# The weight ring of the experts: two lent slots given up, four kept

## The chip, the cores and the metric

One core of a Trainium2 chip runs the whole program. The metric is the device time of one execution in microseconds (us); less is better.

## The reference, cut to what matters

The program computes two transformer-like blocks over 512 tokens of width 1024. The first block has two layers, and each layer ends in an expert stage:

```python
def expert_choice_moe(h, w_router, w_gate, w_up, w_down):
    cap = EC_FACTOR * s // N_EXPERTS                 # 2 * 512 // 16 = 64 tokens for each expert
    logits = jnp.einsum('bsd,de->bse', h, w_router)
    aff = jax.nn.softmax(logits, axis=-1)
    gates, idx = lax.top_k(aff.transpose(0, 2, 1), cap)
    xs = h[b_ix, idx]                                # 64 tokens of each of the 16 experts
    a = jnp.einsum('becd,edf->becf', xs, w_gate)     # 1024 x 1024, float32
    u = jnp.einsum('becd,edf->becf', xs, w_up)       # 1024 x 1024
    y = jnp.einsum('becf,efd->becd', jax.nn.silu(a) * u, w_down)   # 1024 x 1024
    y = y * gates[..., None]
    return jnp.zeros_like(h).at[b_ix, idx].add(y)
```

Each expert has three matrices of 1024 x 1024 in float32, 4 MB each: a layer reads 16 x 3 x 4 MB = 192 MB (of 2^20 bytes) of expert weights, and each weight serves only 64 tokens. The other stages of the program (projections, attention, a recurrent mixer, a long convolution, a feed-forward net) are not touched by the change.

## The kernel before, in words

**Weights come in pieces.** `weight_pieces` writes down all weights of the first block in the order of their use, in pieces of at most 2048 KB. An expert has six pieces: two of `w_gate`, two of `w_up`, two of `w_down`; here they are called G0, G1, U0, U1, D0, D1. A layer has 96 of them. Experts are counted from 0 to 15.

**A ring holds them.** `Ring` (line 51) owns `RING` = 4 slots of 16 KB in each partition, one piece to a slot. `feed` (line 76) runs on SP, the engine whose queue issues the loads. For each next piece it takes the slot whose last piece is the oldest, waits until that piece is used, and issues the load:

```python
s = min((s for s in range(len(self.tiles)) if i < self.until[s]), key=lambda s: self.last[s])
if self.last[s] >= self.fed:
    break
if self.last[s] >= 0:
    sp.wait_ge(self.used, self.last[s] + 1)
sp.dma_start(self.tiles[s][:, 0:src.shape[1]], src).then_inc(self.landed[s], 16)
```

So the loads are issued strictly in the order of the pieces, and a stage's `feed` goes on to the pieces of the next stage as far as the slots let it. `take` makes TensorE wait until a piece has landed; `done` raises `used` with the last matmul that reads the piece.

**Two slots are lent.** The expert stage (`Experts.run`, line 1378) allocates `LENT` = 2 further tiles `lent_weights` and hands them to the ring with `ring.lend(lent, ring.fed + 6 * NE)` (line 1390), until the 96 pieces of the layer are through. With six slots and six pieces to an expert, D0 and D1 always fall into the lent tiles, and G0 to U1 into the ring's own. When the stage begins, the own four slots have already been filled by the stage before (G0 to U1 of expert 0).

**What TensorE does in an expert** (its order is written out by hand in `run`): G0 (`project`, line 1476), the spreading of the places (line 1468), G1, then U0 and U1 and, between them, the put-back of the previous expert's rows (line 1509), the turn of the hidden rows (line 1484), D0 (`down`, line 1495), then the picks of the next group's tokens (line 1451), then D1. Experts come in groups of four. The picks for the next group are spread over a group: two blocks of picks in its first expert, three in the second and third, none in the fourth, which has the slot columns (line 1460) in their place. The last group has neither. Before the first expert the stage has a part that needs no expert weights: softmax, choice of the 64 tokens on VectorE, and the picks of the first group.

After layer 0's experts, the next stage (`chain`, lines 438 to 584) takes the pieces of `w_in` of layer 1. After layer 1's experts the first ring ends; the second block has a ring of its own, `weight_ring_second`, with `RING_2` = 2 slots.

Of the kernel before, what the change touches and what calls it, by code (L numbers as in the profile page):

```python
# [43 lines left out]
CHUNK = 64  # L44
NCH = T // CHUNK
DECAY = -math.exp(-0.5)
RING, RING_2, LENT = 4, 2, 2
SLOT_COLS = 512


# [2890 lines left out]
```

## Time and profile before

| | us |
|---|---|
| median of three runs | 4118.49 (4117.94 to 4123.21) |
| the profiled execution, its own time | 4114.72 |
| its span in the profile | 4113.4 |
| expert weights of layer 0 in use by TensorE | about 523 to 978 |
| expert weights of layer 1 in use by TensorE | about 1493 to 1948 |

TensorE is busy for 86% of the span. The DMA engines are busy for 37% of it on the average, but unevenly: nearly all in two stretches, those of the expert weights. The table's last two lines are positions in the profiled execution, counted from the start of the span.

### The profile page before, as it was taken

How to read it: one execution, taken by the hardware profiler on the slowest of the kernel's cores; microseconds unless marked ns; L12 is line 12 of the kernel's file. 1: busy time of each engine (PE TensorE's matmuls, PEld its weight loads, DVE VectorE, ACT ScalarE, POOL GpSimd, SP SyncE). 2: the span in 40 equal slices, each digit the busy share in tenths (PEclk: the TensorE clock that was granted, in tenths of full speed). 3: DMA queues.
4: the chain of work that ended last, by engine and by line, in shares of the span. 5: the costliest groups of instructions: out<-in, count | busy, mean ns of one | idle time of the engine just before them, and what ended most of it. 6: DMA issues, size and time to landing. Idle time of an engine off the chain costs nothing. (4 is left out here: it accounts for less than half of the span.)

```text
span 4113.4 us, 54317 instructions
## 1 busy us (share of the span) xinstructions
PE 3528.7 (86%) x22946; PEld 2340.4 (57%) x22946; DVE 1963.4 (48%) x2907; ACT 1113.0 (27%) x1839; POOL 310.6 (8%) x248
## 2 busy tenths in 40 slices
PE   7689799998689979998777666578999998789998
PEld 6377443334457643332556555435888776368887
DVE  3655423224365432322455665525764542867645
ACT  3343200002163310000321222112433421554333
POOL 1010000000010000000102332000000100210000
PEclk9899899999899989999888777879999998899999
DMA  5021289997113159998220000001222221422221
GB/s 193 11 103 62 84 366 427 427 428 302 53 42 116 49 224 427 427 428 375 104 78 3 2 2 2 2 33 67 103 103 87 78 103 44 63 76 102 83 92 72
DMA packets 79487, 600.99 MB, mean 146 GB/s; under 512 B 35304, under 2 KB 36584, under 8 KB 43981
## 3 DMA queue, kind: packets, MB, share of 16 engines
q1 hardware_dynamic: 79244, 597.51, 37.0%
q8 instruction: 182, 2.98, 0.3%
q14 instruction: 61, 0.49, 0.0%
HBM read 595.39 MB, written 2.10 MB: 145 GB/s over the span
## 5 line engine op out<-in xcount | busy, mean ns | idle before, releaser
L574 PE MATMUL psum<-source_hi,weights_hi 128*128 128x512 f32 (+1 forms) x2352 | 923.2, 393 | 105.1 <-DVE weights_lo L486 81.0
L574 PE MATMUL psum<-source_lo,weights_hi 128*128 128x512 f32 (+1 forms) x2352 | 913.2, 388 | 0.0
L574 PE MATMUL psum<-source_hi,weights_lo 128*128 128x512 f32 (+1 forms) x2352 | 911.9, 388 | 0.0
L574 PEld LDWEIGHTS psum<-source_hi,weights_hi 128*128 128x128 f32 x2352 | 449.7, 191 | 207.2 <-DVE weights_lo L486 96.2
L574 PEld LDWEIGHTS psum<-source_lo,weights_hi 128*128 128x128 f32 x2352 | 450.3, 191 | 90.0 <-issue 2.7
L574 PEld LDWEIGHTS psum<-source_hi,weights_lo 128*128 128x128 f32 x2352 | 449.6, 191 | 90.2
L1476 PE MATMUL psum<-weight_ring_first,branches 128*64 128x512 f32 x2048 | 465.5, 597 | 16.4 <-DMA weight_ring_first<-in_w_gate 8.6
L486 DVE TENSOR_TENSOR weights_lo<-weight_ring_second,weights_hi 128x1024 fp32r<-128x1024 f32 (+3 forms) x230 | 285.4, 1245 | 301.2 <-ACT weights_hi L441 301.1
L1476 PEld LDWEIGHTS psum<-weight_ring_first,branches 128*64 128x64 f32 x2048 | 138.0, 137 | 304.7 <-issue 270.8
L441 ACT CAST weights_hi<-weight_ring_second 128x1024 fp32r<-128x1024 f32 (+3 forms) x230 | 228.3, 997 | 267.5 <-PE psum L574 244.7
L1627 DVE TENSOR_TENSOR x<-psum,x 128x512 f32<-128x512 f32 x256 | 164.1, 684 | 202.2 <-PE psum L1509 202.2
L1495 PE MATMUL psum<-lent_weights,hidden_t 128*64 128x512 f32 x1024 | 233.7, 598 | 3.3 <-DMA lent_weights<-in_w_down 1.6
L486 DVE TENSOR_TENSOR weights_lo<-weight_ring_first,weights_hi 128x1024 fp32r<-128x1024 f32 (+2 forms) x112 | 140.4, 1269 | 168.4 <-ACT weights_hi L441 168.4
L538 POOL TENSOR_TENSOR sums_of_squares<-squares 128x512 f32<-128x512 f32 (+1 forms) x16 | 25.5, 1596 | 2079.1 <-ACT squares L459 2079.1
L2267 ACT ACTIVATE convolved<-before_convolution,columns 128x512 f32<-128x512 f32 x88 | 71.9, 817 | 277.2 <-DVE before_convolution L2264 277.2
L441 ACT CAST weights_hi<-weight_ring_first 128x1024 fp32r<-128x1024 f32 (+2 forms) x112 | 111.0, 1011 | 131.7 <-PE psum L574 124.3
L1495 PEld LDWEIGHTS psum<-lent_weights,hidden_t 128*64 128x64 f32 x1024 | 67.9, 136 | 135.8 <-issue 109.6
L1987 PE MATMUL psum<-rwkv_scratch 64*64 64x64 f32 x3584 | 114.6, 227 | 22.4 <-POOL rwkv_scratch L1978 22.4
L1987 PEld LDWEIGHTS psum<-rwkv_scratch 64*64 64x64 f32 x3584 | 113.9, 144 | 23.1 <-POOL rwkv_scratch L1978 22.9
L574 PE MATMUL psum<-weights_hi,source_hi 128*128 128x256 f32 x384 | 110.7, 288 | 10.0 <-DVE weights_lo L486 10.0
L2264 DVE TENSOR_TENSOR before_convolution<-psum,roots 128x512 f32<-128x512 f32 x100 | 68.9, 689 | 103.4 <-PE psum L574 103.3
L574 PE MATMUL psum<-weights_hi,source_lo 128*128 128x256 f32 x384 | 110.0, 286 | 0.0
(359 smaller groups left out, 4584.5 us busy)
## 6 DMA issues: line engine op xcount, KB each, us to landing
weight_ring_first<-in_w_gate SPq DMA_DIRECT2D x64, 2048.0 KB, 18.0
weight_ring_first<-in_w_up SPq DMA_DIRECT2D x64, 2048.0 KB, 19.1
lent_weights<-in_w_down SPq DMA_DIRECT2D x64, 2048.0 KB, 18.2
weight_ring_second<-in_ffn_w_up SPq DMA_DIRECT2D x22, 2048.0 KB, 8.0
weight_ring_first<-in_xattn_w_kv SPq DMA_DIRECT2D x8, 2048.0 KB, 8.1
weight_ring_second<-in_ffn_w_down SPq DMA_DIRECT2D x8, 2048.0 KB, 8.0
weight_ring_first<-in_w_in SPq DMA_DIRECT2D x6, 2048.0 KB, 24.4
weight_ring_second<-in_mix_w_in SPq DMA_DIRECT2D x6, 2048.0 KB, 8.0
```

Source lines behind the costliest of these rows:

```text
L441: act.copy(self.whi[:, 0:len(unit.ks), unit.slot * P:unit.slot * P + unit.cols], self.ring.view(unit.piece)[:, :, unit.c0:unit.c0 + unit.c ...
L486: ins = dve.tensor_tensor(lo, self.ring.view(unit.piece)[:, :, unit.c0:unit.c0 + unit.cols], hi.bitcast(F32), ALU.subtract)
L538: pool.tensor_tensor(total, square(q) if m == 1 else total, square(q + m), ALU.add).then_inc(self.added, 1)
L574: ins = pe.matmul(ps, a, b, start=k == 0 and q == 0, stop=k == job.rows // P - 1 and q == 2)
L1476: ins = pe.matmul(psum[HALF * half:HALF * half + HALF, which, :], self.xs[:, k, e // GROUP % 2, e % GROUP * CAP:(e % GROUP + 1) * CAP], w[ ...
L1495: ins = pe.matmul(psum[HALF * half:HALF * half + HALF, self.ROWS, :], hid_t[:, k, part * HALF:(part + 1) * HALF], w[:, k, half * 512:half ...
L1627: dve.tensor_tensor(x, psum[:, bank(), :], x, ALU.add).then_inc(misc_free, 1)
L1987: ins = pe.matmul(K.psum[r, bank + d, c], w[d][r, lhs, c], w[d][r, rhs, c], start=True, stop=True)
L2264: return dve.tensor_tensor(self.raw[:, m % 3, :], ps, r[0], ALU.mult)
L2267: act.activation(self.to(m), self.raw[:, m % 3, :], ACT.Identity, bias=self.b[:, m:m + 1], scale=self.w[1][:, m:m + 1]).then_inc(self.cent ...
```

## The change

The ring borrows nothing any more. `lent` becomes an empty list, `lend` does nothing, and all pieces go through the four own slots. In the expert stage the load of a piece waits for the piece four places before it, where it waited for the one six places before it; and the loads of D0 and D1 of expert 0, which needed no wait, now wait for G0 and G1.

```diff
-RING, RING_2, LENT = 4, 2, 2
+RING, RING_2, LENT = 4, 2, 0
```

Nothing else is edited: every engine's order of computing instructions stays as it is.

## Rows read from the trace of the kernel before

**Rows 1.** The page: span, TensorE, and GB/s in 40 equal slices.

```profile
span 4113.4 us, 54317 instructions
...
GB/s 193 11 103 62 84 366 427 427 428 302 53 42 116 49 224 427 427 428 375 104 78 3 2 2 2 2 33 67 103 103 87 78 103 44 63 76 102 83 92 72
```

**Rows 2.** The page's DMA issues: count, KB each, median us to landing.

```profile
lent_weights<-in_w_down SPq DMA_DIRECT2D x64, 2048.0 KB, 18.2
```

**Rows 3.** Busy time by stretch: us, PE, PEld, DVE, ACT, POOL, PEclk, DMA share, GB/s.

```profile
500.00:520.00 20.00, 9.82 (x59) 9.74 (x60) 12.46 (x26) 0.00 (x0) 0.00 (x0) 0.58 0.00 1
540.00:560.00 20.00, 19.48 (x94) 7.49 (x96) 3.69 (x6) 1.74 (x3) 0.00 (x0) 1.00 1.01 429
800.00:900.00 100.00, 97.75 (x522) 36.52 (x520) 26.27 (x42) 6.43 (x11) 0.00 (x0) 1.00 1.01 428
900.00:950.00 50.00, 44.01 (x204) 13.93 (x202) 13.76 (x21) 3.46 (x6) 0.00 (x0) 1.00 1.01 428
```

**Rows 4.** Timeline of SP's queue, layer 0: start, us, line, load, count.

```profile
486.82 0.91 SPq L84 DMA_DIRECT2D lent_weights<-in_w_down  x2
526.79 4.96 SPq L84 DMA_DIRECT2D weight_ring_first<-in_w_gate  x2
...
553.31 4.96 SPq L84 DMA_DIRECT2D weight_ring_first<-in_w_gate  x2
562.19 4.58 SPq L84 DMA_DIRECT2D weight_ring_first<-in_w_up  x2
572.35 6.92 SPq L84 DMA_DIRECT2D lent_weights<-in_w_down  x2
582.38 4.96 SPq L84 DMA_DIRECT2D weight_ring_first<-in_w_gate  x2
...
953.57 15.25 SPq L84 DMA_DIRECT2D weight_ring_first<-in_w_in  x4
```

**Rows 5.** Timeline of TensorE in layer 0, early: start, us, line, matmuls, count.

```profile
540.52 3.65 PE L1495 MATMUL psum<-lent_weights,hidden_t 128*64 128x512 f32 x16 [0.68 <-ACT hidden_t L1589]
...
582.27 1.12 PE L1468 MATMUL psum<-place_rows,row_selectors 16*128 16x512 f32 x2
...
591.81 3.65 PE L1476 MATMUL psum<-weight_ring_first,branches 128*64 128x512 f32 x16
...
696.30 1.12 PE L1468 MATMUL psum<-place_rows,row_selectors 16*128 16x512 f32 x2
```

**Rows 6.** Timeline of TensorE, experts 14 and 15 of layer 0; in brackets its idle time.

```profile
920.52 3.65 PE L1476 MATMUL psum<-weight_ring_first,branches 128*64 128x512 f32 x16 [1.25 <-DMA weight_ring_first<-in_w_gate]
...
949.88 3.65 PE L1476 MATMUL psum<-weight_ring_first,branches 128*64 128x512 f32 x16 [1.24 <-DMA weight_ring_first<-in_w_gate]
...
974.59 3.65 PE L1495 MATMUL psum<-lent_weights,hidden_t 128*64 128x512 f32 x16 [0.23 <-DMA lent_weights<-in_w_down]
```

**Rows 7.** The same view, D1 of expert 15 in layer 1.

```profile
1944.84 3.65 PE L1495 MATMUL psum<-lent_weights,hidden_t 128*64 128x512 f32 x16 [0.20 <-DMA lent_weights<-in_w_down]
```

**Rows 8.** Ring and lent slots' loads issued in 520:560, in that order.

```profile
DMA to landing us min/median/max: 8.1/11.2/12.2
DMA to landing us min/median/max: 10.6/10.8/11.0
```

**Rows 9.** Lent slots' loads issued in 560:600, ring slots' in 600:650 and 900:950.

```profile
DMA to landing us min/median/max: 10.9/11.8/12.6
...
DMA to landing us min/median/max: 12.9/14.5/16.3
...
DMA to landing us min/median/max: 25.6/25.6/25.9
```

**Rows 10.** Waits in 840:880, those for a DMA: us in total, times, longest.

```profile
PEld psum L1476 <- DMA weight_ring_first<-in_w_up: 0.4, 1, 0.4
```

**Rows 11.** Timeline after the experts of layer 0, ScalarE: the next stage's first cast.

```profile
986.49 1.03 ACT L441 CAST weights_hi<-weight_ring_first 128x1024 fp32r<-128x1024 f32 x1
```

## The prediction, on record before the run

> **What bounds the kernel now.** I read the page first, for where the DMA engines matter at all. Its line of GB/s has two plateaus at 427 to 428, each about five slices of 103 us wide, and elsewhere mostly under 200 [rows 1]. The plateaus are the two expert stages; the change can act only there, for only there are slots lent [rows 2].
>
> Second, the busy times by stretch [rows 3]. In every stretch from 540 us on, the DMA share is 1.01 and the rate 428 or 429: the DMA engines are full from the first expert to the last. TensorE is nearly full too at 800:900, but at 900:950 it is busy for only 44 of 50 us. From 500 to 520 the DMA engines do nothing: all slots are full and the tokens are still being chosen.
>
> Third, the timeline of TensorE at both ends of the stage [rows 5, 6]. The places of expert 2 are spread at 582.27 and those of expert 6 at 696.30: a group of four takes 114.03 us, and TensorE waits for no load in it. The list of waits shows the first, of 0.4 us, only in 840:880 [rows 10]. In the last group, which has no picks, G0 of experts 14 and 15 start at 920.52 and 949.88, each behind a wait for its load. So an expert takes 29.36 us there, and a piece 29.36 / 6 = 4.893 us: that is the DMA engines' pace, to be read off TensorE. Four experts at this pace are 117.4 us. TensorE alone is 3.4 us a group faster; it begins with a stock of pieces landed ahead, eats it up over the first three groups, and is held by the loads in the last. D1, the last piece, starts at 974.59 behind a wait of 0.23 us for its landing; in layer 1 the same stands at 1944.84, with 0.20 us [rows 6, 7]. **The end of both expert stages is thus the landing of the 96th piece**, and that is set by when the stream begins and how many pieces it still has to carry.
>
> **The change, part by part.**
>
> *The head start.* Before, D0 and D1 of expert 0 are issued at 486.82 and land in the idle time; six pieces lie ready when G0 starts. The next load is issued at 526.79, when G0 is used [rows 4]. From then the stream carries 96 - 6 = 90 pieces of the layer. After the change D0 and D1 can't be issued at 486.82. The load at 526.79 is then D0's, the next is D1's, and the stream carries 92 pieces. Two pieces more at 4.893 us are **9.79 us** for a layer, and 19.57 us for both. The idle time at 500:520 can't take them back, since no slot is free.
>
> *Does TensorE wait for D0 of expert 0?* It needs it at 540.52 [rows 5]. The first load of the stream lands in 8.1 us (the minimum [rows 8]), at 534.9. Nothing is lost here.
>
> *Does a ring of four keep the DMA engines full?* SP issues a load in the moment a piece is used; the timeline gives those moments. A row of two loads starts with the first, and the second starts at the row's end less its own 0.33 us. For expert 1: G0 553.31, G1 557.94, U0 562.19, U1 566.44, D0 572.35, D1 578.94, and expert 2's G0 582.38 [rows 4]. As long as TensorE isn't held, these moments are the same after the change, so the stream is the same too, only with each transfer two pieces further back in the list. A load issued when piece i is used brings piece i+4, and TensorE has the time until it wants i+4. The shortest is for D1 of expert 1: used at 578.94, its slot brings U1 of expert 2, wanted at 591.81 [rows 5], 12.87 us. The transfers issued in 560:600 to the lent slots take at most 12.6 us, those in 600:650 12.9 and more [rows 9]. So the first waits come around 590 to 620 us, in experts 2 and 3, and not at 840. From there on TensorE is held to the DMA engines' pace.
>
> Is that pace still 4.893 us? The engines run dry only if a slot comes free too late. Suppose U1 starts as it lands, at about 562.8 in the moments above. The next three landings of the stream are D0's at 567.7, D1's at 572.6 and G0's at 577.5. D1, delayed by the picks, is used at 578.94, some 6.3 us after it landed. The load that this releases has to land 4 x 4.893 = 19.6 us after D1 did, at 592.2, so it has 13.2 us. A load into an empty queue needs 8.1, and at 540:560, where loads take 10.6 to 12.2 us, the share is already 1.01 [rows 3, 8]. There are at least 5 us in hand at the worst place. Cost: nothing. If this cover were gone, each late release would cost its lateness.
>
> *The wait at the end.* In the last group the loads take 25.6 us now, since six slots queue up before the engines [rows 9]. With four it should be 25.6 - 9.8 = 15.8 us. The queue is shorter and the pace is the same.
>
> *The next stage.* SP's waits change the other loads too. Before, the four pieces of w_in are issued from 953.57 on, behind G0, G1, U0, U1 of expert 15 [rows 4]. Now they wait for U0, U1, D0, D1. The first of them lands right behind D1 of expert 15: that one lands at 974.6 + 9.8 = 984.4, the next at 989.3. The next stage's first cast of it comes at 986.49 [rows 11], moved to 996.3: 7 us of cover. The three others are released by U1, D0 and D1, and come one by one while ScalarE is still at the first; the fourth, released at 984.4 + 3.65 = 988.0, lands 8.1 us after at the earliest. Cost: nothing, with the bound that a late fourth piece would be under 10 us. Nothing else is queued behind SP's waits, for the two small tables are issued ahead of them. In layer 1 no piece follows in this ring.
>
> *The pace itself.* The rate is 429 at the short queue of 540:560 and 428 with the long one of 900:950 [rows 3]. At best the short queue wins 1/428 of 450 us, 1 us a layer; at worst a wait on TensorE costs some tenths at the end. I take neither.
>
> Sum: 4114.72 (the profiled execution; its span is 4113.4, with 1.3 us around it) + 19.57 = 4134.3 us. The median of the runs shown is 3.77 us above the profiled execution, so on that median it is 4118.49 + 19.57 = **4138.1 us**, 0.48% slower.
>
> **The rule that speaks against this.** In the last group the rows show TensorE with a wait for nearly each load though six slots are there [rows 6]. The Trainium skill, "Trainium Kernel Development and Optimization", section "Best Practices", asks for double buffering so that DMA and compute overlap; by it, a ring of four pieces is already twice what is needed, and the sum would be 4118.5. The trace disagrees with its being enough here: loads and matmuls overlap all the way, and the end still moves with the number of pieces that were landed ahead. "SBUF — State Buffer", section "The DMA setup-cost knee", of the Trainium skill gives a lone transfer a fixed cost of about 2 us beside bytes over 436 GB/s; as an estimate from that page that is 6.8 us for 2 MB, where the trace has 8.1. The sum is the same by both.
>
> **The rivals.**
>
> *The two slots are hidden anyway (same).* TensorE's own work would have to end the stage: it would have to be at least 9.8 us behind the loads at D1 of expert 15. The 98% of busy time at 800:900 speaks for it. The waits at all of the last group's experts, and the 0.2 us waits at D1 in both layers, speak against it [rows 6, 7]: there is no slack at the end to put 9.8 us into. It would give 4118.5. The point that decides: the landing of D1 has to lie at least 9.8 us before its use, and it lies at it. This is the case on the other side, not slower; I give it 3%.
>
> *The ring of four runs dry.* If the three picks made one release in each expert come so late that its load finds an empty queue, that load costs 8.1 - 4.9 = 3.2 us more than its share. In 14 experts of a layer that is 45 us, 90 in both: 4138 + 90 = 4228 us. It decides when a piece is used more than 11.5 us after its landing (three landings of 4.9, less the 3.2); the worst I find is 6.3. If only the three or four experts around the start of the waits did it, 3 us each, it would be 4138 + 20 = 4158. 5% for the two.
>
> *The next stage pays too.* If the cast at 996.3 had to wait for pieces of w_in, some 5 us once: 4143. Inside the range, 5%.
>
> *Faster.* A shorter queue would have to raise the rate by 9.8 of 450 us, 2.2%, to 437 GB/s, to break even; the row with the shortest queue shows 429. 1%, for something that I don't see.
>
> **How the numbers follow.** The forecast, 4138, has 86%. A change within 0.2% (8 us) is about what a measurement of this kernel can't tell from none. Slower by more is the forecast with the dry ring and the late next stage: 96%; same 3%, faster 1%. The range: low is the lowest run, 4117.9, plus the sum less the 2 us that a better rate might bring, 4135.5, taken down to 4133 for another chip; high is the highest run, 4123.2, plus 19.6 and the late next stage, 4148.
>
> **What the profile after would show.** No lent_weights. In each layer the first load of the stage 40 us later, at TensorE's first release, and the last D1 9.8 us later than before, at about 984.4. The first wait for a load near 600 instead of 870. Waits for loads in all later groups, of 0.3 to 1.3 us, and experts at 29.36 us each from the second group on. Loads in the last group at 15.8 us, and never under 10 after the first few. The DMA share at 1.01 and 427 to 429 GB/s throughout. The end of the program 19.6 us later, and all between and behind the expert stages as long as before. It would be wrong if the share fell under 1 in the groups with picks (ring dry), or if D1 of expert 15 started without a wait (hidden).

## The result, and the profile after

The changed kernel takes 4139.72 us in the median, the kernel before 4117.40 us over all its runs: a ratio of 1.0052, with a 95% interval of 1.0040 to 1.0064. It is slower, as forecast (4138.1 us, 1.0048). One of its six executions took 8938.04 us, and one of the five of its repeat below 6968.64; the ratios leave these two slow ones out, the medians given hold them, and without them the medians are 4137.98 and 4135.50 us. The profiled execution has its own time of 4136.37 us and this span and rates, the answer to [rows 1]:

```profile
span 4135.0 us, 54317 instructions
...
GB/s 192 11 102 62 43 371 427 427 428 307 72 41 102 62 170 427 427 428 419 102 79 2 2 2 2 3 33 66 102 86 93 87 102 44 63 75 94 90 92 72
```

The plateaus stand at 427 to 428 as before; what changed is their edge. The slice before the first plateau fell from 84 to 43 GB/s and that before the second from 224 to 170, and more is moved behind them: the loads that used to lie in the idle time are in the stream now.

The queue of SP in the changed kernel, layer 0 and then layer 1, in the columns of [rows 4]:

```profile
487.56 0.42 SPq L1427 DMA_DIRECT2D places<-in_places  x1
527.97 4.96 SPq L84 DMA_DIRECT2D weight_ring_first<-in_w_down  x2
...
975.54 15.23 SPq L84 DMA_DIRECT2D weight_ring_first<-in_w_in  x4
...
1507.57 4.96 SPq L84 DMA_DIRECT2D weight_ring_first<-in_w_down  x2
```

Behind the two small tables nothing is issued for 40 us; D0 and D1 of expert 0 go out at TensorE's first releases. In the kernel before, the stream of layer 1 began here:

```profile
1496.15 4.96 SPq L84 DMA_DIRECT2D weight_ring_first<-in_w_gate  x2
```

TensorE in the changed kernel: its first wait for a load in layer 0, G0 of experts 14 and 15, D1 of expert 15, and the same D1 in layer 1, to be held against [rows 5, 6, 7]:

```profile
645.93 3.65 PE L1476 MATMUL psum<-weight_ring_first,branches 128*64 128x512 f32 x16 [0.28 <-DMA weight_ring_first<-in_w_up]
...
932.69 3.65 PE L1476 MATMUL psum<-weight_ring_first,branches 128*64 128x512 f32 x16 [1.24 <-DMA weight_ring_first<-in_w_gate]
...
962.07 3.65 PE L1476 MATMUL psum<-weight_ring_first,branches 128*64 128x512 f32 x16 [1.24 <-DMA weight_ring_first<-in_w_gate]
...
986.75 3.65 PE L1495 MATMUL psum<-weight_ring_first,hidden_t 128*64 128x512 f32 x16 [0.23 <-DMA weight_ring_first<-in_w_down]
...
1965.60 3.65 PE L1495 MATMUL psum<-weight_ring_first,hidden_t 128*64 128x512 f32 x16 [0.20 <-DMA weight_ring_first<-in_w_down]
```

An expert of the last group lasts 962.07 - 932.69 = 29.38 us, and 29.36 before: the same pace, the same gaps of 1.24 us at G0. The last D1 starts 12.16 us later in layer 0 and 20.76 us later in layer 1.

Busy time by stretch, with the columns of [rows 3]:

```profile
500.00:520.00 20.00, 8.63 (x49) 8.55 (x50) 12.95 (x28) 0.00 (x0) 0.00 (x0) 0.55 0.00 1
540.00:560.00 20.00, 18.96 (x92) 7.47 (x94) 2.94 (x6) 1.86 (x3) 0.00 (x0) 1.00 1.01 431
800.00:900.00 100.00, 95.52 (x516) 36.14 (x514) 28.07 (x45) 6.17 (x10) 0.00 (x0) 1.00 1.01 428
900.00:950.00 50.00, 44.33 (x198) 13.67 (x196) 11.28 (x17) 3.13 (x5) 0.00 (x0) 1.00 1.01 428
```

The DMA share is 1.01 in each stretch behind the start, as with six slots. At 800:900 TensorE is busy for 95.5 us and not for 97.8: it is held there now. The granted clock is 1.00 in both. Over 400 us of the first stream, the kernel before and then the changed one, the DMA columns are the same and only TensorE's differ:

```profile
560.00:960.00 400.00, 388.54 (x2017) 143.18 (x2014) 114.95 (x187) 26.04 (x42) 0.00 (x0) 1.00 1.01 427
560.00:960.00 400.00, 381.18 (x1980) 140.75 (x1978) 113.75 (x185) 24.77 (x40) 0.00 (x0) 1.00 1.01 427
```

Times from issue to landing of the loads issued in 600:650 and in 900:950, the answer to [rows 9]:

```profile
DMA to landing us min/median/max: 12.2/14.2/17.2
...
DMA to landing us min/median/max: 14.8/15.8/15.9
```

**Where the 21.6 us of span are.** I take as the length of a stream the time from the first load after expert 0's G0 to the start of the last D1. Layer 0: 974.59 - 526.79 = 447.80 us before, 986.75 - 527.97 = 458.78 after, 10.98 more. Layer 1: 1944.84 - 1496.15 = 448.69 before, 1965.60 - 1507.57 = 458.03 after, 9.34 more. Together 20.3 us. The rest of the program has 1.3 us more: 1.18 ahead of the first stream, -0.74 between the two, 0.84 behind the second.

### The profile page after: what moved, and what is told of

Same layout as the page of the kernel before. It is cut to its first block and busy times, and to the rows that moved or that the text cites. A ratio compares the mean times of both kernels' runs of the same rounds, so it can differ in the third digit from the quotient of the medians.

```text
span 4135.0 us, 54317 instructions
## 1 busy us (share of the span) xinstructions
PE 3533.9 (85%) x22946; PEld 2340.4 (57%) x22946; DVE 1959.9 (47%) x2907; ACT 1113.0 (27%) x1839; POOL 310.7 (8%) x248
## 5 line engine op out<-in xcount | busy, mean ns | idle before, releaser
L1495 PE MATMUL psum<-weight_ring_first,hidden_t 128*64 128x512 f32 x1024 | 233.7, 598 | 3.5 <-DMA weight_ring_first<-in_w_down 1.8
L1495 PEld LDWEIGHTS psum<-weight_ring_first,hidden_t 128*64 128x64 f32 x1024 | 67.8, 136 | 136.1 <-issue 109.6
L574 PE MATMUL psum<-weights_lo,source_hi 128*128 128x256 f32 x384 | 110.0, 287 | 0.0
## 6 DMA issues: line engine op xcount, KB each, us to landing
weight_ring_first<-in_w_gate SPq DMA_DIRECT2D x64, 2048.0 KB, 15.8
```

The costliest lines, as they stand in the source:

```text
L574: ins = pe.matmul(ps, a, b, start=k == 0 and q == 0, stop=k == job.rows // P - 1 and q == 2)
L1495: ins = pe.matmul(psum[HALF * half:HALF * half + HALF, self.ROWS, :], hid_t[:, k, part * HALF:(part + 1) * HALF], w[:, k, half * 512:half ...
```

## The experiments

The theory: the end of an expert stage is the landing of its last piece; the DMA engines are full from TensorE's first release on; so each piece that isn't loaded in the idle time ahead costs 4.9 us a layer. Rivals: four slots are too shallow to keep the engines full, or each wait of TensorE costs something in itself. All eight kernels of the experiments were timed in five rounds beside the kernel before, the first four in one set and the last four in another; the first row of the table has the ratio of the result above. The sum of the two streams is 447.80 + 448.69 = 896.5 us for the kernel before and 458.78 + 458.03 = 916.8 for the changed one.

| kernel | ratio to before (95%) | sum of both streams, us | over before |
|---|---|---|---|
| kernel before | 1 | 896.5 | 0 |
| changed kernel | 1.0052 (1.0040 to 1.0064) | 916.8 | 20.3 |
| the same again | 1.0047 (1.0033 to 1.0060) | 918.5 | 22.0 |
| one lent slot | 1.0029 (1.0019 to 1.0040) | 907.6 | 11.1 |
| six slots, no head start | 1.0048 (1.0034 to 1.0061) | 915.2 | 18.7 |
| four slots, four halves in expert 8 | 1.0017 (1.0008 to 1.0025) | 902.1 | 5.6 |
| four slots, halves spread | 1.0001 (0.9992 to 1.0010) | 899.0 | 2.5 |
| lent for two loads only | 1.0034 (1.0023 to 1.0044) | 911.1 | 14.7 |
| six slots, shared tiles | 1.0002 (0.9993 to 1.0011) | 897.6 | 1.1 |
| three lent slots | 0.9970 (0.9959 to 0.9981) | 888.8 | -7.7 |

**The changed kernel again.** No edit.

> The changed kernel once more, beside the kernels of this call. Theory (the end of an expert stage is the landing of its last piece, and two pieces more have to be carried after the first release): 19.6 us slower than before, ratio 1.0048; from the first load after expert 0's G0 to the last D1 458 to 459 us in each layer, where six slots have 448. Rival (the measured 1.0052 came from the chip or from work outside the expert stages): a ratio within 0.2% of 1.

Measured: 4136.07 us, ratio 1.0047 (1.0033 to 1.0060). The loss is reproduced, and the rival falls. In layer 1 the stream is 458.2 us (1512.23 to 1970.42), in layer 0 460.4 (530.84 to 991.19). The same kernel had 458.8 there, so one profile tells a stream's length to some 1.6 us. In layer 0 of the repeat one row differs: U0 of expert 15 waits 2.13 us for its load and its matmuls take 5.35 us in place of 3.65, and D1 then follows D0 without a wait. What delayed that load isn't shown.

**One lent slot.**

```diff
-RING, RING_2, LENT = 4, 2, 2
+RING, RING_2, LENT = 4, 2, 1
```

> One lent slot in place of two: five pieces lie ready when expert 0 starts. Theory: one piece of 4.9 us more in each stream than with two, so 9.8 us slower than before, ratio 1.0024, and D1 of expert 15 4.9 us later than with two lent slots in each layer; loads of the last group take 20.7 us. Rival (a ring of four has its loss from too few transfers in flight, and five are enough): ratio within 0.0005 of 1 and no shift of D1.

Measured: 4128.33 us, ratio 1.0029 (1.0019 to 1.0040), the interval holding the 1.0024 of the theory and not the rival's 1.000. SP's first loads of the two streams, and the last D1 of both layers:

```profile
525.16 0.33 SPq L84 DMA_DIRECT2D weight_ring_first<-in_w_down  x1
...
1501.41 0.33 SPq L84 DMA_DIRECT2D weight_ring_first<-in_w_down  x1
```

```profile
979.17 3.65 PE L1495 MATMUL psum<-weight_ring_first,hidden_t 128*64 128x512 f32 x16 [0.24 <-DMA weight_ring_first<-in_w_down]
...
1955.00 3.65 PE L1495 MATMUL psum<-weight_ring_first,hidden_t 128*64 128x512 f32 x16 [0.20 <-DMA weight_ring_first<-in_w_down]
```

454.0 and 453.6 us, 6.2 and 4.9 more than with two lent slots. The price goes by the piece: about half the loss for half the slots. The load of the lent slot goes out alone here, at 485.19 behind the two small tables, with no other for 40 us. Its time to landing:

```profile
DMA to landing us min/median/max: 8.1/8.1/8.1
```

**Six slots without the head start.** The lent slots are told that they last held the stage's first piece, so their first loads wait until it is used.

```diff
 def lend(self, tiles, until):
-        self.tiles[self.own + i], self.last[self.own + i], self.until[self.own + i] = tile, -1, until
+        self.tiles[self.own + i], self.last[self.own + i], self.until[self.own + i] = tile, self.fed, until
```

> Six slots as before, but the two lent ones stay empty until expert 0's G0 is used; the depth of the ring is that of before from then on, only the two pieces that were loaded in the idle time are missing. Theory (head start): as slow as four slots, 19.6 us over before, ratio 1.0048, and 458 us from the first load to the last D1. Loads of the last group at 25.6 us as with six slots. Rival (depth of the queue): as fast as before, ratio 1.000.

Measured: 4136.11 us, ratio 1.0048 (1.0034 to 1.0061), the number of the theory. SP's queue at the start of layer 0's stream (three loads at once, as two slots more come free with the first piece), then the loads issued in 600:650, their time to landing:

```profile
526.48 0.33 SPq L84 DMA_DIRECT2D weight_ring_first<-in_w_down  x1
526.86 0.43 SPq L84 DMA_DIRECT2D lent_weights<-in_w_down  x1
527.33 0.43 SPq L84 DMA_DIRECT2D lent_weights<-in_w_gate  x1
```

```profile
DMA to landing us min/median/max: 22.2/23.1/24.8
```

Loads take 23.1 us at 600:650, where the kernel before has 14.5 and the changed one 14.2: two pieces more are queued before the engines. And nothing is won by it. This is the run that separates the two things that a lent slot does: more depth than four slots have is worth nothing here, the load in the idle time is worth the whole difference. The streams are 458.1 and 457.1 us. In layer 0 D1 follows D0 without a wait here too, behind a row of U0 of 5.35 us; in layer 1 it waits 0.19 us for its load.

**Four slots and two pieces' worth of bytes fewer.** The four loads of gate and up weights of expert 8 bring half of their bytes; the other half of the slot keeps older weights, so expert 8 is computed partly with stale ones. TensorE's work is whole.

```diff
+            cut = src.shape[1] // 2 if i in self.halved else src.shape[1]
-            sp.dma_start(self.tiles[s][:, 0:src.shape[1]], src).then_inc(self.landed[s], 16)
+            sp.dma_start(self.tiles[s][:, 0:cut], src[:, 0:cut]).then_inc(self.landed[s], 16)
...
             ring.lend(lent, ring.fed + 6 * NE)
+            ring.halved += tuple(ring.fed + 6 * 8 + j for j in range(4))
```

> Four slots, and the four loads of expert 8's gate and up weights bring only half of their bytes (the other half of the slot keeps what lay there, so expert 8 is computed with partly stale weights): the stream carries two pieces' worth less, as with the head start. TensorE does all its matmuls. Theory (the number of bytes between the first release and the last landing sets the end): D1 of expert 15 back where it was with six slots, 448 us after the first load, and the time of before, ratio 1.000 within 0.0007. Rival (the ring of four loses time at late releases or in each wait of TensorE): most of the 19.6 us stay, ratio 1.003 to 1.005.

Measured: 4122.81 us, ratio 1.0017 (1.0008 to 1.0025), between the two expectations, and neither holds: 14.7 us of stream came back, 5.6 stayed. The trace shows where. Busy time at 740:760, and the shortest, median and longest time to landing of the loads issued in 750:800:

```profile
740.00:760.00 20.00, 19.72 (x150) 7.95 (x150) 6.18 (x13) 1.77 (x3) 0.00 (x0) 1.00 0.94 364
```

```profile
DMA to landing us min/median/max: 6.5/10.1/12.3
```

The halved loads brought the stream 9.8 us ahead of TensorE at once. Four slots can't hold such a lead: no slot came free in time, the queue ran short, and the DMA share fell to 0.94. That is the dry ring of the prediction, brought about by the edit. (The 6.5 us is a halved load's, issued at 751.3; the whole piece behind it, issued at 754.7, took 8.1.)

**The same bytes taken where TensorE can follow.** Only G0 of experts 11 to 14 is halved (those four are computed with partly stale gate weights).

```diff
-            ring.halved += tuple(ring.fed + 6 * 8 + j for j in range(4))
+            ring.halved += tuple(ring.fed + 6 * e for e in (11, 12, 13, 14))
```

> Four slots, two pieces' worth of bytes fewer once more, now taken where TensorE is held by the loads and can catch up by 3.2 us an expert: only G0 of experts 11, 12, 13 and 14 is loaded by half (these experts are computed with partly stale gate weights). In the run before this one the four halved loads stood together in expert 8, the time to landing fell to 6.5 us there and the DMA share to 0.94: the ring ran dry and 5.6 of 20 us stayed. Theory: with the cuts spread the queue never empties, the DMA share stays at 1.01, and all of the two pieces comes back: 448 us from the first load to the last D1, ratio 1.000 (0.9993 to 1.0010). Rival (the rest of 5.6 us is a loss of four slots in itself): ratio 1.0013 or more.

Measured: 4118.13 us, ratio 1.0001 (0.9992 to 1.0010). With four slots, and with TensorE's waits and late releases in place up to the first halved load, taking two pieces' worth of bytes out of the stream gives the time of the kernel before. Behind expert 11 most of the waits are gone with the bytes: at 900:950 TensorE is busy for 49.2 us, where the changed kernel has 44.3. So for the waits ahead of it this run shows no cost; those behind it aren't tested by it. By the streams 2.5 us of 20.3 remain, 1.9 in layer 0 and 0.6 in layer 1, where two profiles of one kernel differed by 1.6 in a layer; the rival's 1.0013 is outside the interval.

**Lent slots for two loads only.** The lent slots take D0 and D1 of expert 0 and are given back.

```diff
-            ring.lend(lent, ring.fed + 6 * NE)
+            ring.lend(lent, ring.fed + 6)
```

> The two lent slots carry D0 and D1 of expert 0 and nothing more; from the seventh piece on all goes through the own four. So the head start of before is there and the depth isn't: the load of piece 10 is released by piece 6 and not by piece 4, some 9 us later than with six slots, when the queue is already empty. Theory (a head start lasts only if slots hold it): between the two: 86 pieces behind a load issued at about 553 end at 978, 3 us later than before, and some holes of 1 to 3 us while the queue is short; 8 to 12 us slower in all, ratio 1.0020 to 1.0030, with a DMA share under 1 between 545 and 600. Rival A (only the head start counts): ratio 1.000. Rival B (only the depth counts): ratio 1.0048.

Measured: 4131.22 us, ratio 1.0034 (1.0023 to 1.0044): between the two rivals, as the theory has it, but 14 us and not 8 to 12. SP's queue (D0 and D1 in the idle time, the first release, and the load of piece 10), and the busy time of the hole:

```profile
487.69 0.91 SPq L84 DMA_DIRECT2D lent_weights<-in_w_down  x2
527.59 4.96 SPq L84 DMA_DIRECT2D weight_ring_first<-in_w_gate  x2
...
554.10 4.96 SPq L84 DMA_DIRECT2D weight_ring_first<-in_w_down  x2
```

```profile
550.00:560.00 10.00, 10.00 (x46) 3.14 (x44) 2.06 (x4) 1.27 (x2) 0.00 (x0) 1.00 0.51 180
...
540.00:560.00 20.00, 19.32 (x94) 7.60 (x96) 3.02 (x6) 1.86 (x3) 0.00 (x0) 1.00 0.73 292
560.00:580.00 20.00, 19.72 (x106) 8.41 (x104) 6.65 (x12) 0.84 (x2) 0.00 (x0) 1.00 1.00 408
580.00:600.00 20.00, 19.73 (x94) 6.52 (x92) 7.25 (x11) 1.60 (x3) 0.00 (x0) 1.00 1.00 420
```

Between the fourth load of the stream, issued near 539, and 554.10 none is issued, and the DMA share is 0.51 in 550:560: 5 us of the engines are gone there alone, where I had put the whole loss at 4 to 6 a layer. It is 7.3 a layer by the streams: 7.0 in layer 1 and 7.7 in layer 0, where the bytes account for it: the kernel before moved 429, 429 and 427 GB/s in the three stretches of 20 us, so this one is behind by 6.4, 1.0 and 0.3 us of transfer. Of the head start's 20.3 us only 5.6 are left; the rest was lost for want of slots to keep it in.

**Room for a third lent slot.** It needs 16 KB a partition. Five tiles of 2 KB now share memory with others: the last square and the running count with the SiLU gate, the affinity rows with the hidden rows, the turned hidden rows with the sum of squares, and the row of ones is a broadcast (GpSimd's fill of ones goes to another tile). This kernel still lends two.

```diff
-            square = K.sbuf(ctx, "last_square", [P, T])
+            gated = K.sbuf(ctx, "silu_gate", [P, 512])
+            hid = K.sbuf(ctx, "hidden", [P, 512])
+            hid_t = self.total[:, :].rearrange("p (j s) -> p j s", j=4)
+            square, count, rows = gated, gated[0:NE, :], hid[0:NE, :]
+            ones_row = K.ones[0:NE, 0:1].to_broadcast([NE, T])
...
-            rows = K.sbuf(ctx, "affinities_t", [NE, T])
-            count = K.sbuf(ctx, "chosen_so_far", [NE, T])
...
-            ones_row = K.sbuf(ctx, "ones_rows", [NE, T])
...
-            gated = K.sbuf(ctx, "silu_gate", [P, 512])
-            hid = K.sbuf(ctx, "hidden", [P, 512])
-            hid_t = K.sbuf(ctx, "hidden_t", [P, 4, P])
...
-                pool.memset(ones_row[:, :], 1.0).then_inc(ones_made, 1)
+                pool.memset(place_t[:, 0, :], 1.0).then_inc(ones_made, 1)
```

> Control for the next kernel: six slots as before, but five small tiles of the expert stage share memory with others whose life doesn't overlap, and the row of ones is a broadcast of a constant. All theories: the time of before, ratio 1.000 within 0.0008.

Measured: 4118.66 us, ratio 1.0002 (0.9993 to 1.0011). The sharing costs nothing that can be seen.

**Three lent slots.** On top of the shared tiles:

```diff
-RING, RING_2, LENT = 4, 2, 2
+RING, RING_2, LENT = 4, 2, 3
```

> The same with three lent slots, seven in all, which the shared tiles make room for: seven pieces lie ready when expert 0 starts. Theory: one piece fewer behind the first release, 4.9 us a layer, as TensorE is still held in the last group with six slots: 9.8 us faster than before, ratio 0.9976; 443 us from the first load to the last D1, and 30.5 us to landing in the last group. Rival (six slots were enough, the loss of four was in the depth): ratio 1.000. A second rival: TensorE's own pace sets the end before the whole 4.9 us are won: 0.9980 to 0.9995.

Measured: 4106.51 us, ratio 0.9970 (0.9959 to 0.9981), faster than both kernels. The median is 10.0 us under that of the kernel before, 4116.47, in the same set. SP's queue in layer 0 (three loads in the idle time, then the first release) and in layer 1, and the last D1 of both layers:

```profile
491.86 0.91 SPq L84 DMA_DIRECT2D lent_weights<-in_w_down  x2
492.81 0.43 SPq L84 DMA_DIRECT2D lent_weights<-in_w_gate  x1
530.42 0.33 SPq L84 DMA_DIRECT2D weight_ring_first<-in_w_gate  x1
...
1498.03 0.33 SPq L84 DMA_DIRECT2D weight_ring_first<-in_w_gate  x1
```

```profile
975.48 3.65 PE L1493 MATMUL psum<-lent_weights,sum_of_squares 128*64 128x512 f32 x16 [0.22 <-DMA lent_weights<-in_w_down]
...
1941.79 3.65 PE L1493 MATMUL psum<-lent_weights,sum_of_squares 128*64 128x512 f32 x16 [0.18 <-DMA lent_weights<-in_w_down]
```

Its loads to the ring's own slots issued in 900:950, time to landing:

```profile
DMA to landing us min/median/max: 28.2/31.3/32.1
```

The queue is one piece longer than with six slots (31.3 us against 25.6), near the 30.5 expected. The streams are 445.1 and 443.8 us, 7.7 us shorter in all than with two lent slots and 8.7 shorter than in its control, for an expected 9.8. D1 still starts behind a wait for its load, so TensorE's own pace isn't the bound yet: that speaks against the second rival of this run, of whose range the interval holds only the edge (0.9980 to 0.9981). It holds the 0.9976 of the theory too.

## Why the prediction was right

**The bound.** That the landing of the 96th piece ends the stage was the base of it all, read from two waits of 0.2 us [rows 6, 7]. It stands: more loads in the idle time bring the end forward, fewer put it back, and bytes taken from the stream bring it forward at an unchanged ring. The rate over 560:960 is 427 GB/s before and after, so what grew is what the stream carries. D1 of expert 15 waited for its load in both layers of every profile but two, where the load had landed some 0.6 and 0.8 us ahead of it in layer 0 (the repeat, and six slots without the head start).

**The head start, 19.6 us.** Measured 20.3 by the streams in the profile (10.98 and 9.34), 18.7 to 22.0 over the three kernels that lack it. The medians of the executions differ by 20.6 us (4137.98 less 4117.40). The last D1 of layer 0 is at 986.75 where 984.4 was forecast: 1.2 us of that lie ahead of the stream and 1.2 in it. The size of the term is right within what one profile repeats to. The other 1.3 us of the span lie outside the streams. That they belong to the change isn't shown; the repeat has its first release 2.9 us later than the changed kernel's (530.84 against 527.97), so such shifts come without an edit.

**D0 of expert 0.** No wait for it: TensorE's first wait in layer 0 is the one at 645.93.

**A ring of four keeps the engines full.** The share is 1.01 in the stretches above. The other side, a dry ring, was shown to exist in two experiments: in expert 8 with its halved loads, share 0.94, where the first whole piece landed in 8.1 us, and where a release came 15 us after the one before it, share 0.51. In the changed kernel the shortest time to landing behind the start is 11.9 us, in 560:600.

**The place of the first wait was wrong.** I had put it at 590 to 620 us, in experts 2 and 3, and it is at 645.93, at U0 of expert 4. In the repeat it is at U1 of expert 3:

```profile
625.30 3.65 PE L1476 MATMUL psum<-weight_ring_first,branches 128*64 128x512 f32 x16 [0.23 <-DMA weight_ring_first<-in_w_up]
```

So the same program moves it by some 20 us, and both places are later than forecast. The term that failed is the time to landing of the load that D1's use releases. I compared its 12.87 us of room with the 12.9 of the ring's own slots in 600:650 [rows 9]; but a load that is issued late finds less before it, and the shortest room meets the shortest times. In the changed kernel D1 of expert 1 released its load at 580.12, and it took 11.9 us; that of expert 2, released at 609.18, took 12.2. In the repeat the latter took 13.1, more than the room, and there is the wait. The place of the first wait doesn't enter the sum, because the loads end the stage wherever TensorE catches up with them.

**The pace of the middle groups.** I had put experts at 29.36 us each from the second group on. The places of experts 4, 8 and 12 are spread at 640.28, 758.62 and 877.66 us, so these two groups take 118.3 and 119.0 us, and not 117.4; only the last group goes at 29.38 an expert. The rate is 427 GB/s in 640:760 and in 760:880. Why TensorE takes 0.9 and 1.6 us more than the loads' pace there isn't shown.

**The loads at the end.** 15.8 us was forecast for the last group, and the median is 15.8 (the answer above).

**The next stage.** The four loads of w_in go out from 975.54 on, 22.0 us later than the 953.57 of [rows 4], and the first cast:

```profile
998.63 1.03 ACT L441 CAST weights_hi<-weight_ring_first 128x1024 fp32r<-128x1024 f32 x1
```

It comes 12.14 us after that of [rows 11], as much as D1 (12.16). The cover of 7 us was enough, and the cost is nothing.

**The rivals.** "Hidden anyway" fell with the first measurement. The rule of the Trainium skill, "Trainium Kernel Development and Optimization", section "Best Practices", to double-buffer so that loads and compute overlap, is true of these kernels and doesn't price them: overlap was complete with four, six and seven slots, and the times differ by 0.8%. Another rule, in "Perfetto Trace Analysis", section "Optimization Strategy", of the Trainium skill, reads a gap that repeats, on the engine that should be saturated, as a possible sign of too little room for buffers. Here TensorE's gap of 1.24 us at each G0 of the last group is the same with six slots and with four. It is the DMA engines' pace against TensorE's. That slots help all the same comes from what they hold before the stream begins.

## What to carry to other kernels

Where a stage ends with a wait on its last load and the transfer engines are full, count what still has to be moved after they start, and divide by the rate. A buffer is worth what it lets you load before that start, and only as long as it stays lent: its depth in the steady state was worth nothing here, where the queue never ran short. Check that side too: with the head start and too few slots to keep it in, 14.7 of the 20.3 us were lost again. To tell the two apart, keep the number of buffers and delay their first filling.

## What the runs showed of the hardware beyond what was expected

The rate doesn't depend on how much is queued, once enough is: 426 to 431 GB/s in the stretches of the kernel before and the changed one, though their loads of 2 MB took from some 11 to 26 us to land, and 429 in 900:950 with three lent slots, where they took up to 32. Below that the rate falls. A load of 2 MB with nothing else queued took 8.1 us. Where the loads of the kernel with slots lent for two loads took 8.7 to 11.8 us, 408 and 420 GB/s were moved in 560:580 and 580:600, at a share of 1.00: the share alone doesn't show this loss. It went to 0.94 and 0.51 in the two stretches in which the ring of four had run short.
